# A hybrid decoder step: the state-space convolutions get a buffer of their own, and the norm of the conformer output moves two tiles forward

## The chip, the cores and the metric

One core of a Trainium2 chip. The core has five engines with a queue each: PE (TensorE, matrix products), DVE (VectorE), ACT (ScalarE), POOL (GpSimd) and SP (SyncE, which here only starts transfers). They run side by side and wait for each other through semaphores; each works through its own queue strictly in the order in which the program wrote it. The metric is the device time of one launch in microseconds, lower is better; a kernel's time is the median of its runs.

## What is computed

Two layers (`DEPTH = 2`) of a decoder trunk, over 1024 prompt positions and 8 sequences of 4 sample positions (1056 columns in all). The part around the change:

```python
u = x @ params['w_in'][l]
z, xbc, dt_raw, q, k, v, qi, ki, wi, glu = jnp.split(u, points, axis=-1)
xbc, ssd_conv_new = causal_dwconv(xbc, ssd_conv_prev, ssd_conv_w, ssd_conv_b)   # 4 taps, 768 channels
xbc = jax.nn.silu(xbc)
...
idx, valid = index_select(qi, wi, ki, q_pos, k_top)                             # the best 256 keys of each query
...
gl = glu[..., :CC_WIDTH] * jax.nn.sigmoid(glu[..., CC_WIDTH:])
c, cc_conv_new = causal_dwconv(gl, cc_conv_prev, cc_conv_w, cc_conv_b)          # 31 taps, 256 channels
y_cc = jax.nn.silu(layer_norm(c, cc_ln_g, cc_ln_b))
```

State-space scan, sparse attention, an output projection, two layer norms and a gated feed-forward with a width-3 convolution make up the rest of a layer.

## The kernel before

Activations stay in on-chip memory with channels on the 128 partitions, so a tile is 128 channels by 1056 columns. A layer is a row of stages with a barrier between them (`Stages.end`). The change lies in the third stage, which I call **the projection stage**. In it PE computes 20 tiles of `x @ w_in`, written out as a list of jobs (`IN_ORDER`, `JOBS`, lines 102 to 112):

- two gate and two GLU tiles (gate, GLU, gate, GLU), the input of the conformer convolution;
- XBC0 to XBC5, the input of the state-space ("SSD") convolution;
- Z0 to Z3, the gate of the state-space output;
- K0, K1, Q0, Q1, each followed one tile later by a `rot` job (a product with a rotation matrix, three instructions), which the rotary embedding needs;
- V0 and V1.

Two more jobs belong to the conformer's layer norm: `mean` (a product with a matrix of 1/256) and `var` (the same of the squares). Their places in the list are what lines 105 to 108 decide.

**Two sets of banks.** Job n writes one of two sets of accumulation banks (`n % 2`). PE may start job n only when job n-2 has been read out (`await_freed(pe, n - 2)`). Who reads it out: ACT for XBC, Z, K and Q tiles, DVE for V tiles (two copies) and for `rot` (`rotate`, lines 1678 to 1686: three DVE instructions) and `mean` (`norm_centre`, two subtractions), ACT for `var`.

**What DVE and ACT do beside it.** In the same stage the 256 best keys of each query are found by binary search, 31 bits (`choose`). For each bit DVE finishes the bit before (L1913, L1914), makes the next trial (L1906, L1907), counts two of the sets itself (L1860 to L1910), and ACT counts the other five (L1435). DVE cannot finish a bit before ACT's five counts are done. `BITS_OF_JOB` puts two bits on each tile from the first gate to K0, and one on K1. On ACT the two bits stand behind the tile's read-out.

**Convolutions.** `convolve_by_taps` makes one DVE instruction per tap (L1666 for the first tap, L1668 for the others). The SSD convolution of a tile (4 taps, 1080 columns) is put into `inline` and runs between the tile's two bits. The conformer convolution (`convolve_conformer`, two tiles, 31 taps of 1296 columns) is put into `aside`, a list of work cut into steps. `spend(us, steps)` takes steps from it until their estimated cost (1.35 us a tap, from its width) has used up a budget: 3 after each bit that has no inline work, and at the end of a tile 4 in the XBC and Z tiles. After K1 `aside` holds the rest of the key choice, with 5, 11 and 6 at the end of the later tiles.

**The shared buffer.** The SSD convolutions accumulate in `ACC[1]`, and so does the second conformer tile. Therefore `convolve_conformer` only yields empty steps until Z0 (`ssd_convolved`), and waits for the last SSD `silu`.

On ACT the `mean` job is four activations that add the conformer's bias (L1358, L1359), then two squares (L1274); the `var` job is a square root (L1325), and two activations (L1330) after DVE's reciprocal and scaling (`norm`, L1608, L1612).

Of the kernel before, what the change touches and what calls it, by code (L numbers as in the profile page):

```python
# [24 lines left out]
ACT = mybir.ActivationFunctionType  # L25
AX = mybir.AxisListType

D_MODEL, SEQ, DEPTH, DEC_BATCH, DEC_SEQ, PAST_LEN, PAGE = 1024, 1024, 2, 8, 4, 2048, 128
HEAD, SSD_HEADS, SSD_STATE, SSD_W = 64, 8, 64, 4
# [72 lines left out]
IN_ORDER = [T_GATE, T_GLU, T_GATE + 1, T_GLU + 1] + list(range(T_XBC, T_GATE)) + list(range(T_Z, N_IN))  # L102
for _j in IN_ORDER:

    if _j == T_V:
        JOBS.append(("mean", "cc"))
    if _j == T_V + 1:
        JOBS.append(("var", "cc"))
    JOBS.append(("in", _j))
    if _j - 1 in (T_K, T_K + 1, T_Q, T_Q + 1):  # L110
        JOBS.append(("rot", _j - 1))
# [67 lines left out]
def build(nc, xT, w_in, w_out, w_up, w_down, vec, ln0, const, pages, cache_k, cache_v, cache_kidx,  # L179
          ssm_in, ssd_in, cc_in, ffn_in, yT, kT_out, v_out, ki_out, ssm_p, ssm_s, ssd_out, cc_out, ffn_out):  # L180
    ctx = ExitStack()
    with ctx:
# [33 lines left out]
        def v(col, rows=slice(0, P)):  # L216
            return VEC[rows, col:col + 1]
# [3 lines left out]
        def view(*dims, parts=False):  # L221
            n = int(np.prod(dims))
            a = (WORK_PARTS if parts else WORK)[:, at[0]:at[0] + n]
            at[0] += n
            assert at[0] <= WORK_SIZE, at[0]
            if len(dims) == 2:
                return a.rearrange("p (a b) -> p a b", a=dims[0])
            if len(dims) == 3:
                return a.rearrange("p (a b c) -> p a b c", a=dims[0], b=dims[1])
            return a  # L230
# [38 lines left out]
        at[0] = qi_at  # L269
        ROPE2 = view(TOK)  # L270
        SSDO, CCO = view(6, SSD_H * (1 + DEC_BATCH)), view(2, CC_H * (1 + DEC_BATCH))
        ACC = [MIX[:, 4:6, :].rearrange("p a b -> p (a b)")[:, 0:CC_LEN], view(CC_LEN)]
        assert at[0] <= common

# [222 lines left out]
        def samples(a, seg_len, first, n):  # L497

            return a.rearrange("p (b s) -> p b s", s=seg_len)[:, :, first:first + n]
# [749 lines left out]
        def _(act):  # L1249
# [85 lines left out]
            with act.Fori(0, DEPTH) as layer:  # L1335
# [8 lines left out]
                def silu_xbc(t):  # L1344

                    act.wait_ge(conv_done, t + 1)
                    act.wait_ge(saved, t + 3)
                    act.activation(XBC[:, t, 0:SEQ], ACC[1][:, 0:SEQ], ACT.Silu, bias=v(V_SSDB + t))
                    act.activation(by_sample(XBC[:, t, SEQ:TOK]),
                                   samples(ACC[1][:, SSD_S0:SSD_S0 + DEC_BATCH * SSD_SEG], SSD_SEG, 0, DEC_SEQ),  # L1350
                                   ACT.Silu, bias=v(V_SSDB + t)).then_inc(silu_done, 1)

                def project(n):
# [239 lines left out]
        def _(dve):  # L1593
# [62 lines left out]
            with dve.Fori(0, DEPTH) as layer:  # L1656
# [6 lines left out]
                def convolve_by_taps(acc, src, taps, col, done):  # L1663

                    w = acc.shape[-1]
                    step.then_wait(dve.tensor_scalar(acc, src[:, 0:w], v(col), None, ALU.mult))  # L1666
                    for k in range(1, taps):
                        ins = dve.scalar_tensor_tensor(out=acc, in0=src[:, k:k + w], scalar=v(col + k), in1=acc,  # L1668
                                                       op0=ALU.mult, op1=ALU.add)
                        if k < taps - 1:  # L1670
                            step.then_wait(ins)
                            yield w / 960
                    ins.then_inc(done, 1)
# [11 lines left out]
                                                            op0=ALU.mult, op1=ALU.mult))  # L1685
                    dve.tensor_tensor(raw, raw, ROPE, ALU.add).then_inc(free[n % 2], 1)

                aside, inline, ssd_convolved = [], [], []

                def spend(us, steps):  # L1690

# [6 lines left out]

                def convolve_conformer():
                    for t in range(2):  # L1700
                        while t and not ssd_convolved:
                            yield 1.0
                        if t:
                            dve.wait_ge(silu_done, 6)
                        await_freed(dve, JOB[("in", T_GLU + t)])
                        yield from convolve_by_taps(ACC[t][:, 0:CC_LEN - CC_H], CC[:, t, :], CC_W, V_CCW + t * CC_W,
                                                    cc_convolved)

                def project(n):
# [24 lines left out]
                    elif name[0] == "dup":  # L1734
                        await_full(dve, n)
                        dve.tensor_tensor(KID, job_psum(n), c("cos"), ALU.mult).then_inc(free[n % 2], 1)
                    elif name[0] == "rotdup":
                        await_full(dve, n)
                        dve.tensor_tensor(ROPE1, job_psum(n), c("sin"), ALU.mult).then_inc(free[n % 2], 1)
                        await_freed(dve, n)  # L1740
                        await_freed(dve, n - 1)
                        step.then_wait(dve.tensor_tensor(KID, KID, ROPE1, ALU.add))
                    elif name[0] == "turn":
                        await_full(dve, n)
                        for rows, ch, a, w in ((P, slice(0, NCHUNK), 0, NCHUNK * P),
                                               (NS, slice(NCHUNK, NCHUNK + 1), NCHUNK * P, P)):
                            t = job_psum(n, w, slice(0, rows), first=a).rearrange("p (c m) -> p c m", m=P)
                            dve.tensor_copy(DTT[0:rows, ch, :], t[:, :, DT_ROW:DT_ROW + SSD_HEADS])
                            ins = dve.tensor_scalar(WIT[0:rows, ch, :], t[:, :, WI_ROW:WI_ROW + IDX_HEADS],
                                                    IDX_HEADS ** -0.5, None, ALU.mult)  # L1750
                        ins.then_inc(free[n % 2], 1)
                    elif name[0] == "rot":
                        r = name[1]
                        await_freed(dve, JOB[("in", r)])
                        rotate(QI[:, r - T_QI, :] if r < T_XBC else KTL[:, r - T_K, :] if r < T_Q
                               else QT[:, r - T_Q, :], n, ROPE1 if r < T_XBC else ROPE2,
                               ATT_SCALE if T_Q <= r < T_V else 1.0)
                    elif T_XBC <= name[1] < T_GATE:
                        t = name[1] - T_XBC
                        await_freed(dve, n)  # L1760
                        if t:
                            dve.wait_ge(silu_done, t)
                        inline.append(convolve_by_taps(ACC[1][:, 0:SSD_LEN - SSD_H], XBC[:, t, :], SSD_W,
                                                       V_SSDW + t * SSD_W, conv_done))
                    elif T_GLU <= name[1] < T_Z:
                        t = name[1] - T_GLU
                        await_full(dve, n)
                        if t == 0:
                            dve.wait_ge(hist_set, 1)
                        await_freed(dve, JOB[("in", T_GATE + t)])  # L1770
                        dve.tensor_tensor(CC[:, t, CC_H:CC_S0], job_psum(n, SEQ), MIX[:, 6 + t, 0:SEQ], ALU.mult)
                        dve.tensor_tensor(samples(CC[:, t, CC_S0:], CC_SEG, CC_H, DEC_SEQ),
                                          by_sample(job_psum(n, NS, first=SEQ)), by_sample(MIX[:, 6 + t, SEQ:TOK]),
                                          ALU.mult).then_inc(free[n % 2], 1)
                        if t == 0:
                            aside.append(convolve_conformer())
                    elif name[1] >= T_V:
                        t = name[1] - T_V
                        await_full(dve, n)
                        dve.tensor_copy(VTOK[:, 0:NCHUNK, t * P:(t + 1) * P],  # L1780
                                        job_psum(n, SEQ).rearrange("p (c m) -> p c m", m=P))
                        dve.tensor_copy(VTOK[0:NS, NCHUNK, t * P:(t + 1) * P],
                                        job_psum(n, P, slice(0, NS), first=SEQ)).then_inc(free[n % 2], 1)
# [184 lines left out]
                for n in range(N_IDX, N_A):  # L1968
                    project(n)
                    if JOBS[n][0] == "in":  # L1970
                        j = JOBS[n][1]
                        if j == T_GATE:
                            while next(chosen):
                                pass
                        search(j)
                        if j == T_Z:
                            ssd_convolved.append(True)
                        if j == LAST_BITS:
                            aside.append(chosen)
                        spend(4 if j < T_K else 0 if j == T_K else 5 if j < T_Q else 11 if j < T_V else 6, aside)  # L1980
                stage.end()


# [456 lines left out]
```

## Time and profile before

| | before |
|---|---|
| median of three runs | 3820.9 us (3813.37, 3820.9, 3825.1) |
| the profiled execution | 3816.51 us, its span 3814.7 us |
| PE busy | 3304.1 us, 87% of the span |
| DVE busy | 1909.9 us, 50% |
| ACT busy | 1236.7 us, 32% |
| mean granted clock of PE | 0.919 of full speed |

Busy time is an average over stages with different limits. PE at 87% says that most of the launch is bound by products; the projection stage, about 370 us in each of the two layers, is one in which PE, DVE and ACT take turns in waiting. The profiled execution lies 4.4 us below the median of the runs. In the rows below, a timeline row has start, duration, engine, line, operation, result and inputs, shape and count; the bracket is the idle time of the engine ahead of it and who ended it.

### The profile page before, as it was taken

To read this page: it belongs to the slowest core of one execution; us is meant where nothing else is said; L and a number is where in the kernel's file an instruction comes from. 1 tells how busy PE (TensorE), PEld (TensorE's weight loads), DVE (VectorE), ACT (ScalarE), POOL (GpSimd) and SP (SyncE) were. 2 spreads that over 40 slices of the span, in tenths; PEclk is the share of its full clock that TensorE was granted. 3 is DMA by queue.
4 is the path that set the end of the run, shared out by engine and by line. 5 is a ranking of instruction groups with operands and counts; after the bars stand their busy time and mean duration, and the time that the engine had idled before them with its cause. 6 is when DMAs were issued, how large, how long until landed. Compare 5 with 4: busy or idle time off the path is not lost.

```text
span 3814.7 us, 51646 instructions
## 1 busy us (share of the span) xinstructions
PE 3304.1 (87%) x19286; PEld 2652.2 (70%) x19286; DVE 1909.9 (50%) x2976; ACT 1236.7 (32%) x2251; POOL 638.6 (17%) x651
## 2 busy tenths in 40 slices
PE   4899887857889999999868998786669999999995
PEld 2454455624789999999834453564349899999994
DVE  4467864332475434334435868633226645335335
ACT  3246623333252112212223574243333412112213
POOL 0000000001013333333100000000110333334331
PEclk8999998857999999999989998897589999999998
DMA  3111104304301111111021110142151111111111
GB/s 100 49 36 29 32 17 124 94 17 123 102 17 35 52 48 37 53 50 34 27 81 48 34 34 23 62 117 63 35 155 40 34 45 36 54 45 37 55 34 58
DMA packets 169894, 206.59 MB, mean 54 GB/s; under 512 B 61025, under 2 KB 138146, under 8 KB 168738
## 3 DMA queue, kind: packets, MB, share of 16 engines
q1 hardware_dynamic: 143138, 185.36, 16.4%
q10 hardware_dynamic: 26496, 17.84, 1.6%
q8 instruction: 154, 2.52, 0.3%
q14 instruction: 106, 0.87, 0.1%
HBM read 187.17 MB, written 15.96 MB: 53 GB/s over the span
## 4 chain that ended last, share of the span: by engine, by line
PE 64%; DVE 16%; ACT 9%; SPq 5%; issue 3%; DMA 2%; POOL 0%; ACTq 0%; DVEq 0%; POOLq 0%
PE PS L742 41%; PE PS L723 7%; DVE WORK L1668 4%; DVE MIX L1668 2%; ACT WORK L1435 2%; PE PS L755 2%; PE PS L827 2%; ACT X L1306 2%; SPq L424 2%; SPq L425 2%; DVE WORK L1860 1%; PE PS L935 1%; DMA RING<-cache_k 1%; PE PS L781 1%; DVE WORK L1632 1%
## 5 line engine op out<-in xcount | busy, mean ns | idle before, releaser
L742 PE MATMUL PS<-WORK_parts,WHIGH_parts 128*128 128x352 f32 x4224 | 869.5, 328 | 35.2 <-POOL WORK_parts L709 17.7
L723 PE MATMUL PS<-X,RING 128*128 128x512 f32 (+1 forms) x2016 | 671.8, 496 | 109.3 <-DMA RING<-w_in 65.4
L742 PEld LDWEIGHTS PS<-WORK_parts,WHIGH_parts 128*128 128x128 f32 x4224 | 724.2, 191 | 38.9 <-issue 20.6
L742 PE MATMUL PS<-WORK_parts,RING_parts 128*128 128x352 f32 x3168 | 691.3, 327 | 0.0
L723 PEld LDWEIGHTS PS<-X,RING 128*128 128x128 f32 x2016 | 338.4, 194 | 443.8 <-issue 375.2
L742 PEld LDWEIGHTS PS<-WORK_parts,RING_parts 128*128 128x128 f32 x3168 | 545.4, 190 | 0.0
L1668 DVE SCALAR_TENSOR_TENSOR WORK<-WORK,VEC 128x1072 f32<-128x1072 f32 (+2 forms) x272 | 525.6, 1932 | 9.7
L1252 ACT ACTIVATE WORK<-PS 128x32 f32<-128x32 f32 (+11 forms) x412 | 190.8, 514 | 842.1 <-PE PS L742 579.7
L489 POOL TENSOR_TENSOR RING_parts<-RING,WHIGH_parts 128x1024 fp32r<-128x1024 f32 (+2 forms) x184 | 372.0, 2022 | 467.2 <-ACT WHIGH_parts L1252 466.9
L742 PE MATMUL PS<-X_parts,WHIGH_parts 128*128 128x352 f32 x2016 | 434.4, 323 | 0.0
L1435 ACT ACTIVATE WORK<-WORK 128x512 bf16<-128x512 f32 x310 | 285.7, 922 | 198.5 <-DVE WORK L1907 198.4
L1666 DVE TENSOR_SCALAR WORK<-WORK,VEC 128x1072 f32<-128x1072 f32 (+2 forms) x102 | 80.0, 784 | 529.8 <-ACT WORK L1252 529.4
L742 PEld LDWEIGHTS PS<-X_parts,WHIGH_parts 128*128 128x128 f32 x2016 | 344.4, 188 | 0.0
L1252 ACT ACTIVATE WHIGH_parts<-RING 128x1024 fp32r<-128x1024 f32 (+2 forms) x188 | 155.5, 827 | 442.6 <-PE PS L742 420.0
L2264 DVE TENSOR_TENSOR MIX<-MIX,PS 128x1056 f32<-128x1056 f32 x80 | 100.3, 1253 | 286.9 <-PE PS L742 286.9
L755 PE MATMUL PS<-WORK_parts 128*128 128x352 f32 x576 | 144.2, 330 | 0.0
L2077 DVE CUSTOM_DVE_ANT_0 WORK<-PS,WORK 128x384 f32<-128x384 f32 (+5 forms) x48 | 42.4, 883 | 201.8 <-PE PS L1084 201.8
L709 POOL TENSOR_TENSOR WORK_parts<-WORK,WORK_parts 128x1056 fp32r<-128x1056 f32 x44 | 108.3, 2462 | 167.6 <-ACT WORK_parts L1252 167.6
L1252 ACT ACTIVATE WORK_parts<-WORK 128x1056 fp32r<-128x1056 f32 (+1 forms) x56 | 59.4, 1078 | 217.9 <-DVE WORK L2252 217.9
L935 PE MATMUL PS<-CONST,RING 128*128 128x128 f32 x512 | 83.0, 305 | 49.5 <-DMA RING<-cache_k 30.7
L1860 DVE TENSOR_SCALAR_CACHE_REDUCE WORK<-WORK 128x544 bf16<-128x544 f32 (+6 forms) x164 | 115.9, 742 | 0.3
L935 PEld LDWEIGHTS PS<-CONST,RING 128*128 128x128 f32 x512 | 62.3, 155 | 67.9 <-DMA RING<-cache_k 37.0
(318 smaller groups left out, 3722.2 us busy)
## 6 DMA issues: line engine op xcount, KB each, us to landing
RING<-w_up SPq DMA_DIRECT2D x88, 512.0 KB, 3.6
RING<-cache_k SPq DMA_DIRECT2D x200, 128.0 KB, 2.2
RING<-cache_v SPq DMA_DIRECT2D x192, 128.0 KB, 2.1
RING<-w_in SPq DMA_DIRECT2D x46, 512.0 KB, 3.6
RING<-w_down SPq DMA_DIRECT2D x80, 256.0 KB, 2.7
RING<-cache_v ACTq DMA_DIRECT2D x64, 128.0 KB, 2.5
RING<-cache_k ACTq DMA_DIRECT2D x56, 128.0 KB, 2.6
yT<-X SPq DMA_DIRECT2D x5, 1408.0 KB, 5.5
```

What stands on the lines that cost most here:

```text
L489: eng.tensor_tensor(low, raw, WHIGH[:, m % 2, 0:w].bitcast(F32), ALU.subtract).then_inc(done, 1)
L709: pool.tensor_tensor(HIDL[:, b, :], HID[:, b, :], HIDH[:, b, :].bitcast(F32), ALU.subtract).then_inc(hid_low, 1)
L723: mm = pe.matmul(job_psum(n, w, first=first), stationary(k), moving(k)[:, first:first + w], start=k == 0, stop=k == k_tiles - 1)
L742: mm = pe.matmul(thirds(n)[:, third, :], a, x[:, third * THIRD:(third + 1) * THIRD], start=k == 0 and part == 0, stop=k == tiles - 1 and p ...
L755: mm = pe.matmul(dst, a[:, w], third_of(x, t), start=k == 0 and part == 0, stop=k == KT - 1 and part == 2)
L935: mm = pe.transpose(key_bank(k)[:, (j % 2 * 2 + t) * P:(j % 2 * 2 + t + 1) * P], cache_page(name)[:, j, t * P:(t + 1) * P], c("ident"))
L1252: return act.activation(dst, src, ACT.Copy)
L1435: ins = act.activation(SCAN_ASIDE[s][:, 0:w], SEL[:, SEL_AT[i]:SEL_AT[i] + w], ACT.Sign, bias=SCAN_TRIED[:, s:s + 1], scale=SCAN_SCALE, ac ...
L1666: step.then_wait(dve.tensor_scalar(acc, src[:, 0:w], v(col), None, ALU.mult))
L1668: ins = dve.scalar_tensor_tensor(out=acc, in0=src[:, k:k + w], scalar=v(col + k), in1=acc, op0=ALU.mult, op1=ALU.add)
L1860: marks.append(step.mark(dve.tensor_scalar(ASIDE[len(marks) % 2][:, 0:x.shape[-1]], x, limit, None, op, ALU.add, accum_out=to)))
L2264: dve.tensor_tensor(y, y, thirds(n), ALU.add).then_inc(free[n % 2], 1)
```

## The change

The SSD convolutions accumulate in `SSD_ACC`, a part of `MIX` that is unused until Z2 is read out. The second conformer tile no longer waits: `ssd_convolved` and the wait for `silu_done` are gone. The budget at the end of an XBC tile is 7 instead of 4 (six conformer taps instead of three). `mean` stands ahead of Q0 instead of V0, `var` ahead of Q1 instead of V1. Nothing else changes, but since `n % 2` counts jobs, the moves also change which job's banks a later job waits for.

```diff
--- before.py
+++ after.py
@@ -102,9 +102,9 @@
 IN_ORDER = [T_GATE, T_GLU, T_GATE + 1, T_GLU + 1] + list(range(T_XBC, T_GATE)) + list(range(T_Z, N_IN))
 for _j in IN_ORDER:
-    if _j == T_V:
+    if _j == T_Q:
         JOBS.append(("mean", "cc"))
-    if _j == T_V + 1:
+    if _j == T_Q + 1:
         JOBS.append(("var", "cc"))
     JOBS.append(("in", _j))
     if _j - 1 in (T_K, T_K + 1, T_Q, T_Q + 1):
@@ -269,6 +269,7 @@
         at[0] = qi_at
         ROPE2 = view(TOK)
         SSDO, CCO = view(6, SSD_H * (1 + DEC_BATCH)), view(2, CC_H * (1 + DEC_BATCH))
+        SSD_ACC = MIX[:, 2:4, :].rearrange("p a b -> p (a b)")[:, 0:SSD_LEN]
         ACC = [MIX[:, 4:6, :].rearrange("p a b -> p (a b)")[:, 0:CC_LEN], view(CC_LEN)]
         assert at[0] <= common
@@ -1345,9 +1346,9 @@
                     act.wait_ge(conv_done, t + 1)
                     act.wait_ge(saved, t + 3)
-                    act.activation(XBC[:, t, 0:SEQ], ACC[1][:, 0:SEQ], ACT.Silu, bias=v(V_SSDB + t))
+                    act.activation(XBC[:, t, 0:SEQ], SSD_ACC[:, 0:SEQ], ACT.Silu, bias=v(V_SSDB + t))
                     act.activation(by_sample(XBC[:, t, SEQ:TOK]),
-                                   samples(ACC[1][:, SSD_S0:SSD_S0 + DEC_BATCH * SSD_SEG], SSD_SEG, 0, DEC_SEQ),
+                                   samples(SSD_ACC[:, SSD_S0:SSD_S0 + DEC_BATCH * SSD_SEG], SSD_SEG, 0, DEC_SEQ),
                                    ACT.Silu, bias=v(V_SSDB + t)).then_inc(silu_done, 1)
                 def project(n):
@@ -1685,7 +1686,7 @@
                                                             op0=ALU.mult, op1=ALU.mult))
                     dve.tensor_tensor(raw, raw, ROPE, ALU.add).then_inc(free[n % 2], 1)
-                aside, inline, ssd_convolved = [], [], []
+                aside, inline = [], []
                 def spend(us, steps):
@@ -1698,10 +1699,6 @@
                 def convolve_conformer():
                     for t in range(2):
-                        while t and not ssd_convolved:
-                            yield 1.0
-                        if t:
-                            dve.wait_ge(silu_done, 6)
                         await_freed(dve, JOB[("in", T_GLU + t)])
                         yield from convolve_by_taps(ACC[t][:, 0:CC_LEN - CC_H], CC[:, t, :], CC_W, V_CCW + t * CC_W,
                                                     cc_convolved)
@@ -1760,7 +1757,7 @@
                         await_freed(dve, n)
                         if t:
                             dve.wait_ge(silu_done, t)
-                        inline.append(convolve_by_taps(ACC[1][:, 0:SSD_LEN - SSD_H], XBC[:, t, :], SSD_W,
+                        inline.append(convolve_by_taps(SSD_ACC[:, 0:SSD_LEN - SSD_H], XBC[:, t, :], SSD_W,
                                                        V_SSDW + t * SSD_W, conv_done))
                     elif T_GLU <= name[1] < T_Z:
                         t = name[1] - T_GLU
@@ -1973,11 +1970,9 @@
                             while next(chosen):
                                 pass
                         search(j)
-                        if j == T_Z:
-                            ssd_convolved.append(True)
                         if j == LAST_BITS:
                             aside.append(chosen)
-                        spend(4 if j < T_K else 0 if j == T_K else 5 if j < T_Q else 11 if j < T_V else 6, aside)
+                        spend(7 if T_XBC <= j < T_GATE else 4 if j < T_K else 0 if j == T_K else 5 if j < T_Q else 11 if j < T_V else 6, aside)
                 stage.end()
```

How the order moves on the engines (line numbers of the changed kernel are one higher up to line 1690, three lower behind 1780):

DVE, the end of tile XBC1: behind the second bit's own counts (L1860 to L1910) and ahead of the next tile's first bit (L1913). Before:

```order
L1860 TENSOR_SCALAR WORK<-WORK 128x544 [waits vector_step]
L1860 TENSOR_SCALAR WORK<-WORK 128x384 [waits vector_step]
L1873 STREAM_TRANSPOSE WORK<-WORK 128x32 [waits vector_step]
L1874 TENSOR_REDUCE WORK<-WORK 128x8 [waits vector_step]
L1875 COPY WORK<-WORK 128x32 [waits vector_step]
L1877 STREAM_TRANSPOSE WORK<-WORK 128x32 [waits vector_step]
L1910 TENSOR_TENSOR WORK<-WORK 128x7 [waits vector_step]
L1913 TENSOR_TENSOR WORK<-WORK 128x5 [waits silu_done,scan_counted,bank_set_free0,vector_step]
L1914 COPY_PREDICATED WORK<-WORK 128x7 [waits vector_step]
```

With the change (L1669 is the conformer tap, the others as above):

```order
L1857 TENSOR_SCALAR WORK<-WORK 128x544 [waits vector_step]
L1857 TENSOR_SCALAR WORK<-WORK 128x384 [waits vector_step]
L1870 STREAM_TRANSPOSE WORK<-WORK 128x32 [waits vector_step]
L1871 TENSOR_REDUCE WORK<-WORK 128x8 [waits vector_step]
L1872 COPY WORK<-WORK 128x32 [waits vector_step]
L1874 STREAM_TRANSPOSE WORK<-WORK 128x32 [waits vector_step]
L1907 TENSOR_TENSOR WORK<-WORK 128x7 [waits vector_step]
L1669 SCALAR_TENSOR_TENSOR WORK<-WORK,VEC 128x1296 [waits vector_step] x9
L1910 TENSOR_TENSOR WORK<-WORK 128x5 [waits silu_done,scan_counted,bank_set_free0,vector_step]
L1911 COPY_PREDICATED WORK<-WORK 128x7 [waits vector_step]
```

Nine conformer taps now stand in the queue ahead of XBC2's first bit, where there were none. The same nine stand at the end of XBC2, five at the end of XBC3, and at the end of XBC0 eleven (a first tap, L1667, among them) in place of three; the tiles Z0 to Z3 have none left.

PE, behind the K1 tile. `WORK,CONST` is a `rot` job (the first three rows: that of K0), `X,RING` a projection tile (here Q0), `MIX,MEAN` the job `mean`. Before:

```order
L723 MATMUL PS<-WORK,CONST 128x512 [waits bank_set_free0]
L723 MATMUL PS<-WORK,CONST 128x512
L723 MATMUL PS<-WORK,CONST 128x32
L723 MATMUL PS<-X,RING 128x512 [waits bank_set_free1,slot_loaded1]
L723 MATMUL PS<-X,RING 128x512 x15
L723 MATMUL PS<-X,RING 128x32 x8
L723 MATMUL PS<-WORK,CONST 128x512 [waits bank_set_free0,bank_set_free1]
```

With the change:

```order
L724 MATMUL PS<-WORK,CONST 128x512 [waits bank_set_free0]
L724 MATMUL PS<-WORK,CONST 128x512
L724 MATMUL PS<-WORK,CONST 128x32
L724 MATMUL PS<-MIX,MEAN 128x512 [waits bank_set_free1,cc_ready]
L724 MATMUL PS<-MIX,MEAN 128x512 x3
L724 MATMUL PS<-MIX,MEAN 128x32 x2
L724 MATMUL PS<-X,RING 128x512 [waits bank_set_free0,slot_loaded1]
```

`mean`, which waits for ACT's bias activations (`cc_ready`), now stands ahead of Q0. Q0's banks are those of K0's `rot` (`bank_set_free0`), which DVE frees by rotating; they were those of K1 (`bank_set_free1`), which ACT frees by a copy.

PE, the end of the stage. `RING,X` is a V tile, `L801` the job `var`, the `WORK,CONST` rows are the `rot` job of Q1. Before:

```order
L723 MATMUL PS<-WORK,CONST 128x512 [waits bank_set_free1]
L723 MATMUL PS<-WORK,CONST 128x512
L723 MATMUL PS<-WORK,CONST 128x32
L801 MATMUL PS<-MIX,MEAN 128x512 [waits norm_squared,bank_set_free0]
L801 MATMUL PS<-MIX,MEAN 128x512
L801 MATMUL PS<-MIX,MEAN 128x32
L801 MATMUL PS<-MIX,MEAN 128x512 [waits norm_squared]
L801 MATMUL PS<-MIX,MEAN 128x512
L801 MATMUL PS<-MIX,MEAN 128x32
L827 MATMUL PS<-RING,X 128x128 [waits bank_set_free1,slot_loaded0]
```

With the change:

```order
L828 MATMUL PS<-RING,X 128x128 [waits bank_set_free1,slot_loaded3]
L828 MATMUL PS<-RING,X 128x128 x63
L828 MATMUL PS<-RING,X 32x128 x8
L724 MATMUL PS<-WORK,CONST 128x512 [waits bank_set_free0,bank_set_free1]
L724 MATMUL PS<-WORK,CONST 128x512
L724 MATMUL PS<-WORK,CONST 128x32
L828 MATMUL PS<-RING,X 128x128 [waits bank_set_free1,slot_loaded0]
```

V1 (last row of before, last row with the change) took the banks of Q1's `rot` job, which DVE frees; it now takes those of V0.

## Rows read from the trace of the kernel before

**Rows 1.** Timeline of PE, first layer's projection stage.

```profile
315.02 15.68 PE L723 MATMUL PS<-X,RING 128*128 128x512 f32 x48 [2.29 <-ACT WORK L1252]
...
379.68 62.49 PE L723 MATMUL PS<-X,RING 128*128 128x512 f32 x192 [0.15 <-ACT WORK L1252]
...
445.05 18.05 PE L723 MATMUL PS<-X,RING 128*128 128x512 f32 x48 [2.88 <-ACT MIX L1378]
...
483.75 17.48 PE L723 MATMUL PS<-X,RING 128*128 128x512 f32 x48 [15.44 <-ACT WORK L1252]
...
501.06 2.10 PE L723 MATMUL PS<-WORK,CONST 128*128 128x512 f32 x6
...
522.33 4.07 PE L723 MATMUL PS<-MIX,MEAN 128*128 128x512 f32 x12 [1.70 <-ACT MIX L1359]
...
526.23 16.40 PE L827 MATMUL PS<-RING,X 128*128 128x128 f32 x144
...
556.27 17.73 PE L827 MATMUL PS<-RING,X 128*128 128x128 f32 x144 [7.71 <-DVE WORK L1686]
```

**Rows 2.** Timeline of PE, second layer: Q0 and V1.

```profile
2356.75 17.94 PE L723 MATMUL PS<-X,RING 128*128 128x512 f32 x48 [14.14 <-ACT WORK L1252]
...
2429.73 17.95 PE L827 MATMUL PS<-RING,X 128*128 128x128 f32 x144 [7.71 <-DVE WORK L1686]
```

**Rows 3.** Timeline of DVE in tiles XBC0 to XBC4.

```profile
311.42 4.78 DVE L1668 SCALAR_TENSOR_TENSOR MIX<-WORK,VEC,MIX 128x1296 f32<-128x1296 f32 x3
...
317.64 0.17 DVE L1913 TENSOR_TENSOR WORK<-WORK 128x5 int32<-128x5 f32 x1 [1.45 <-ACT WORK L1349]
...
320.69 0.78 DVE L1666 TENSOR_SCALAR WORK<-WORK,VEC 128x1080 f32<-128x1080 f32 x1
...
325.53 0.15 DVE L1913 TENSOR_TENSOR WORK<-WORK 128x5 int32<-128x5 f32 x1
...
333.48 0.16 DVE L1913 TENSOR_TENSOR WORK<-WORK 128x5 int32<-128x5 f32 x1 [4.94 <-ACT WORK L1349]
...
365.14 0.17 DVE L1913 TENSOR_TENSOR WORK<-WORK 128x5 int32<-128x5 f32 x1 [4.94 <-ACT WORK L1349]
```

**Rows 4.** Timeline of DVE, first bits of tiles Z2 and Z3.

```profile
430.59 0.16 DVE L1913 TENSOR_TENSOR WORK<-WORK 128x5 int32<-128x5 f32 x1
...
451.13 0.17 DVE L1913 TENSOR_TENSOR WORK<-WORK 128x5 int32<-128x5 f32 x1
```

**Rows 5.** Timeline of DVE, from the 31st bit to the stage's end.

```profile
488.39 0.17 DVE L1913 TENSOR_TENSOR WORK<-WORK 128x5 int32<-128x5 f32 x1 [2.60 <-ACT WORK L1435]
...
494.71 1.26 DVE L1682 SCALAR_TENSOR_TENSOR WORK<-WORK,CONST 128x1056 f32<-128x1056 f32 x1
...
556.26 6.75 DVE L1608 RECIPROCAL WORK<-WORK 128x1056 f32<-128x1056 f32 x1
...
574.03 1.22 DVE L1780 COPY WORK<-PS 128x1024 f32<-128x1024 f32 x1 [8.56 <-PE PS L827]
...
585.65 0.63 DVE L1956 TENSOR_SCALAR WORK<-WORK 128x896 f32<-128x896 f32 x1
```

**Rows 6.** Groups by shape: conformer taps of both tiles; busy us, mean ns.

```profile
L1668 DVE SCALAR_TENSOR_TENSOR WORK<-WORK,VEC 128x1296 f32<-128x1296 f32 x60 | 94.2, 1569 | 2.1
...
L1668 DVE SCALAR_TENSOR_TENSOR MIX<-WORK,VEC,MIX 128x1296 f32<-128x1296 f32 x60 | 94.1, 1569 | 2.1
```

**Rows 7.** Timeline of ACT in the same stage.

```profile
378.45 1.08 ACT L1252 ACTIVATE WORK<-PS 128x1024 f32<-128x1024 f32 x2
...
477.97 0.72 ACT L1435 ACTIVATE WORK<-WORK 128x512 bf16<-128x512 f32 x1 [0.92 <-DVE WORK L1907]
...
482.58 1.02 ACT L1252 ACTIVATE WORK<-PS 128x1056 f32<-128x1056 f32 x1
...
519.67 1.14 ACT L1358 ACTIVATE MIX<-MIX,VEC 128x1024 f32<-128x1024 f32 x1
```

**Rows 8.** Windows: from:to, length, busy of PE, PEld, DVE, ACT, POOL, granted clock, DMA.

```profile
445.00:463.00 18.00, 17.95 (x48) 8.86 (x48) 17.20 (x34) 7.89 (x17) 0.00 (x0) 0.87 0.02 7
```

## The prediction

> **What bounds the kernel now.** I read the timeline of PE through the projection stage first, since PE is 87% busy: there only its idle times can be won. Its waits name who held it, and for each of them I went to that engine's timeline.
>
> PE [rows 1]: a projection tile takes 62.49/4 = 15.6 us, a V tile 16.3, a `rot` job 2.0, `mean` and `var` 4.1 each. The first eight tiles run nearly closed up. Then PE waits 2.88 us ahead of K1, 15.44 ahead of Q0 (ended by ACT, which had to finish bits before it could copy K1), 1.70 ahead of `mean` and 7.71 ahead of V1 (DVE had to rotate Q1 first). The second layer has 14.14 and 7.71 at the same places [rows 2].
>
> DVE shows where that comes from. In the XBC tiles it runs 317.64 to 333.48, 15.84 us a tile, and sits idle 4.94 us of it, waiting for ACT [rows 3]; PE, at 15.6, is just behind. In the Z tiles, where the second conformer tile now runs, a tile takes 451.13 - 430.59 = 20.5 us [rows 4], 5 more than PE's; the lateness gathered there is the 15.44 us ahead of Q0. So the limit changes hands: a DVE-ACT loop in the XBC tiles that is as fast as PE, DVE in the Z tiles.
>
> The end of the stage: after V1's product DVE works from 574.03 to 585.65 + 0.63 = 586.28 [rows 5], 12.3 us, and the next stage starts on that. So the stage's length follows V1's end on PE one for one.
>
> **The change, step by step** (first layer, times on the clock of the trace of before).
>
> *The buffer itself.* Taps cost 1569 ns into either memory, so the move of the SSD sums costs nothing [rows 6]; with its gap a tap takes 1.60, a first tap 0.93 (estimated from 0.78 for 1080 columns [rows 3] as 0.78 x 1296/1080).
>
> *The taps pulled into the XBC tiles.* XBC0: DVE had three taps from 311.42 to 316.2, then waited until 317.64. Now a first tap and seven others follow: 316.2 + 0.93 + 7 x 1.60 = 328.3, a lag of 10.7 against before. XBC1 and XBC2: from the first bit to the second 325.53 - 317.64 = 7.89; the second bit 320.69 - 317.64 = 3.05; nine taps 14.4; together 25.3 in place of 15.84, a lag of 9.5 each, because only three of nine taps fit into the 4.94 us of idle time. XBC3 with five taps: 7.89 + 3.05 + 8.0 = 18.9, 3.1 more. The sum is 10.7 + 9.5 + 9.5 + 3.1 = 32.8: XBC4, whose first bit was at 365.14 [rows 3], starts at 397.9. From there on nothing is aside, and the loop is that of before, 32.8 late.
>
> ACT's read-out of XBC5, at 378.45 [rows 7], is what lets Z1 start on PE at 379.68 [rows 1]. ACT's read-outs stand behind the bits in its queue, and the bits wait for DVE's trial. So Z1 starts at 379.68 + 32.8 = 412.5. The PE idle time of this stretch is new: about 12, 8 to 10 and 8 to 10 us ahead of XBC4, XBC5 and Z0 (lags of 10.7, 20.2 and 29.7 at their read-outs), 1 ahead of Z1.
>
> *What the Z tiles give back.* DVE now has only bits there. ACT's counts take 482.58 - 477.97 = 4.61 and wait 0.92 for the next trial [rows 7]: about 5.6 a bit, and 2 x 5.6 + 1.0 for the read-out = 12.3 us, under PE's 15.6. So PE runs Z1, Z2, Z3, K0, K1 closed up: 412.5 + 5 x 15.6 = 490.5 (before: 445.05 + 18.05 = 463.1), K0's `rot` to 492.5.
>
> *The norm two tiles sooner.* ACT reads K1 (1.0), counts the 31st bit (4.6) and adds the bias (519.67 to 522.33, 2.7 [rows 1, 7]): 490.6 + 8.3 = 498.9. `mean` starts there, PE having waited 6.5, and ends at 503.1. On DVE the key choice's step behind the 31st bit stands ahead of K0's rotation: 488.39 to 494.71, 6.3 [rows 5]; then three instructions of 1.26, 3.8 in all. From the end of the 31st count at 496.3 this gives 496.4 + 6.3 + 3.8 = 506.5, and Q0 now needs those banks: it starts at 506.6, PE having waited another 3.5. Before it started at 483.75, so the lag is 22.9: 10 of the 32.8 are back.
>
> *From Q0 to the end.* A wait costs clock. After 2.29 us of idle XBC3 still took 15.68; after 2.88 K1 took 18.05, with a granted clock of 0.87 over 445 to 463 [rows 1, 8]: part of it at the lower level of 1.2 GHz. Q0's 3.5 us is nearest to the second, so I charge 2.2 of the possible 0 to 2.4. Then 506.6 + 17.8 = 524.4; K1's `rot` 526.4; `var` 530.5 (its squares were done by 512); Q1 needs K1's rotation, 526.5 + 3.8 = 530.3, just in time, to 546.1; Q0's `rot` 548.1; V0 564.4; Q1's `rot` 566.4; V1, which needs only V0's copies (1.5 us) and no rotation, 566.4 + 16.3 = 582.7. V0 needs Q1 read out, and ACT is by then in the norm: 530.6 + 1.1 + DVE's reciprocal 6.75 [rows 5] + two scalings 2.5 + two activations 2.4 = 543.4, 2.7 us to spare. In before V1 ended at 556.27 + 17.73 = 574.0. The stage ends 8.7 us later. What is saved here is the 7.71 and 1.70 of waits, and `mean` (4.1), which moved ahead of Q0.
>
> The tail of 12.3 us is unchanged: the budgets behind K1 and the steps they take are the same. POOL's and SP's queues hold the same instructions in the same order.
>
> **The sum.** 8.7 us a layer, twice: +17.4 us on the profiled 3816.5 is 3833.9. That execution lies 4.4 below the median; the four times known average 3819.0, and 3819.0 + 17.4 gives **3836 us**.
>
> The Trainium skill, "TensorE: Matmul & The Clock Gate", section "Part 1: The HAM clock gate (the "warmup" mystery)", says that the array's clock is halved unless recent activity has released it. The loss behind K1's wait agrees [rows 1, 8]; by it the same loss would stand behind every long new wait. That is rival C; where such a start is covered, the sum does not change.
>
> **The rivals.**
>
> *A, faster.* The taps hide in the XBC tiles and the late Z tiles are simply gone. Each us of lag at XBC4 is one us at V1, so break-even is a lag of 32.8 - 8.7 = 24.1, and with no lag the time is 3819 + 2 x (8.7 - 32.8) = 3771. For it: PE's four named waits are 27.7 us a layer. Against it: the idle time in an XBC tile is 4.94 us and the new taps are 14.4; a lag of 24 would need taps of 1.3 us. Chance 0.05.
>
> *B, no difference to speak of.* The waits around `mean` come out shorter: the 6.5 and 3.5 stand in a row on three engines (ACT's count and bias, DVE's step and rotation), and without the 2.2 of clock and some 2 us of these it is +4.5 a layer, 3828. A full loss of these two waits and of the clock, 12.2, would give 3819 - 7 = 3812, still within 0.3%. For it: the 3.5 is a difference of long sums. Against it: each of the orders is fixed by a queue. Chance 0.20.
>
> *C, slower than I say.* The clock is lost at more places: each slow start costs up to 2.4 [rows 1]. In the XBC tiles this is covered, since XBC4 (342.7 + 18.0) ends long before XBC5 may start, and Z0 (393.5 + 18.0 = 411.5) 1 us before Z1; ahead of `mean` it is covered by DVE's rotation, which ends 3.4 us later. If Z0 or V1 fall behind too, it is 2.4 to 4.8 a layer: 3841 to 3846. Chance 0.12.
>
> *D, the norm holds V0.* If DVE reached the reciprocal over 2.7 us late, V0 would slip. Its queue holds only K1's rotation there. It would add what exceeds 2.7; I count it into C.
>
> **Chances and range.** The forecast as worked out, +13 to +20: 0.63. A 0.05, B 0.20, C and D 0.12. What a measurement of this kernel can tell from no change is about 0.3%, 11.5 us. Faster by more than that: A, 0.05. Slower: the forecast, C and D, 0.75, less 0.01 for its edge; within 0.3%: B, and that edge, 0.21. The range leaves out A, the lower half of B and the top of C: 3823 to 3847. Its low end is +4 (the clock unpaid, and B's cut in the waits), its high end C's.
>
> **What would show it.** In the profile of the changed kernel: tiles XBC1 and XBC2 last 25 us on DVE between first bits, with nine taps each; PE waits about 12, 9, 9 us ahead of XBC4, XBC5 and Z0, ended by ACT; the Z tiles run closed up at 15.6; two waits of about 6.5 and 3.5 stand around `mean`; none ahead of V1; V1 ends near 583 and the stage near 595. Wrong would be: XBC tiles of 16 to 18 us, Q0 starting before 500, or a stage that ends before 586. A fault of size would sit first in the 3.5 ahead of Q0 and in the clock behind it.

## The result and the profile after

The changed kernel takes 3833.8 us, the median of 20 runs, against 3818.0 for the kernel before on the same chips: a ratio of 1.0037, 95% interval 1.0027 to 1.0046. It is slower by 10 to 18 us, on the side and at about the size that was forecast (+17.4 us, 3836). The profiled execution took 3835.1 us, its span 3833.3.

PE's timeline in the projection stage, first layer, then second. This execution reaches the stage 1.96 us sooner than that of before (201.94 against 203.90); "aligned" below means that 1.96 is added.

```profile
201.94 108.83 PE L724 MATMUL PS<-X,RING 128*128 128x512 f32 x336 [0.91 <-DVEq L454]
...
340.80 18.05 PE L724 MATMUL PS<-X,RING 128*128 128x512 f32 x48 [12.09 <-ACT WORK L1253]
366.17 17.31 PE L724 MATMUL PS<-X,RING 128*128 128x512 f32 x48 [7.32 <-ACT WORK L1253]
391.53 18.28 PE L724 MATMUL PS<-X,RING 128*128 128x512 f32 x48 [8.05 <-ACT WORK L1253]
410.35 78.00 PE L724 MATMUL PS<-X,RING 128*128 128x512 f32 x240 [0.54 <-ACT WORK L1253]
...
496.57 7.04 PE L724 MATMUL PS<-MIX,MEAN 128*128 128x512 f32 x12 [6.28 <-ACT MIX L1360]
504.43 15.68 PE L724 MATMUL PS<-X,RING 128*128 128x512 f32 x48 [0.82 <-DVE WORK L1687]
...
526.15 15.68 PE L724 MATMUL PS<-X,RING 128*128 128x512 f32 x48 [0.22 <-DVE WORK L1687]
...
561.89 16.40 PE L828 MATMUL PS<-RING,X 128*128 128x128 f32 x144
592.45 0.66 PE L978 MATMUL PS<-WORK,CONST 128*128 128x64 f32 x2 [14.16 <-DVE WORK L1988]
```

```profile
2085.07 108.83 PE L724 MATMUL PS<-X,RING 128*128 128x512 f32 x336 [0.91 <-DVEq L454]
...
2223.94 18.55 PE L724 MATMUL PS<-X,RING 128*128 128x512 f32 x48 [10.69 <-ACT WORK L1253]
...
2293.48 79.45 PE L724 MATMUL PS<-X,RING 128*128 128x512 f32 x240 [1.72 <-ACT WORK L1253]
...
2381.16 6.82 PE L724 MATMUL PS<-MIX,MEAN 128*128 128x512 f32 x12 [6.28 <-ACT MIX L1360]
2389.02 15.68 PE L724 MATMUL PS<-X,RING 128*128 128x512 f32 x48 [1.03 <-DVE WORK L1687]
...
2477.03 0.66 PE L978 MATMUL PS<-WORK,CONST 128*128 128x64 f32 x2 [14.16 <-DVE WORK L1988]
```

The first row of the stage and the first of the next one, in both layers of the kernel before:

```profile
203.90 108.83 PE L723 MATMUL PS<-X,RING 128*128 128x512 f32 x336 [0.91 <-DVEq L453]
...
588.16 0.66 PE L977 MATMUL PS<-WORK,CONST 128*128 128x64 f32 x2 [14.17 <-DVE WORK L1993]
...
2076.92 108.83 PE L723 MATMUL PS<-X,RING 128*128 128x512 f32 x336 [0.92 <-DVEq L453]
...
2461.84 0.66 PE L977 MATMUL PS<-WORK,CONST 128*128 128x64 f32 x2 [14.17 <-DVE WORK L1993]
```

Against [rows 1, 2]: the waits of 15.44 ahead of Q0 and 7.71 ahead of V1 are gone, the tiles Z1 to K1 run closed up, that is without waits (78.00/5 = 15.6), and in place of those waits stand 12.09, 7.32 and 8.05 us ahead of XBC4, XBC5 and Z0 and 6.28 ahead of `mean`. The last row of each layer is the first product of the next stage. From the first gate tile to it, the stage is 592.45 - 201.94 = 390.5 us long, before 588.16 - 203.90 = 384.3; in the second layer 392.0 against 384.9. That is 13.3 us for both layers.

DVE's timeline of the same stretch: first bits of the XBC tiles, with the conformer taps ahead of them.

```profile
326.28 0.16 DVE L1910 TENSOR_TENSOR WORK<-WORK 128x5 int32<-128x5 f32 x1
...
337.20 14.41 DVE L1669 SCALAR_TENSOR_TENSOR WORK<-WORK,VEC 128x1296 f32<-128x1296 f32 x9
351.65 0.17 DVE L1910 TENSOR_TENSOR WORK<-WORK 128x5 int32<-128x5 f32 x1
...
362.57 14.40 DVE L1669 SCALAR_TENSOR_TENSOR WORK<-WORK,VEC 128x1296 f32<-128x1296 f32 x9
377.00 0.16 DVE L1910 TENSOR_TENSOR WORK<-WORK 128x5 int32<-128x5 f32 x1
...
395.83 0.15 DVE L1910 TENSOR_TENSOR WORK<-WORK 128x5 int32<-128x5 f32 x1
...
411.65 0.16 DVE L1910 TENSOR_TENSOR WORK<-WORK 128x5 int32<-128x5 f32 x1 [4.94 <-ACT WORK L1350]
```

XBC1 and XBC2 last 25.4 us each (15.84 in [rows 3]), with nine taps and no idle time left. XBC4, a tile without taps, has its 4.94 back (last row).

Two windows, `mean` and Q0 (length, busy time of PE, PEld, DVE, ACT, POOL, then the granted clock):

```profile
496.50:503.60 7.10, 7.03 (x12) 3.13 (x12) 6.89 (x14) 0.02 (x1) 0.00 (x0) 0.57 0.00 0
504.40:520.00 15.60, 15.57 (x49) 7.95 (x49) 12.12 (x28) 2.17 (x2) 0.00 (x0) 1.00 0.01 1
```

The clock was lost in `mean`, granted 0.57 and so mostly at the lower level of 1.2 GHz; Q0 behind it ran at full speed. The Trainium skill, "TensorE: Matmul & The Clock Gate", section "Part 1: The HAM clock gate (the "warmup" mystery)", says that a clock lowered by idle time is released again by activity; the two windows agree.

### The profile page after: what moved, and what is told of

It is laid out like the page before. It is cut to its first block, busy times and chain, and to the rows that moved or that the text cites. A ratio compares the mean times of both kernels' runs of the same rounds, so it can differ in the third digit from the quotient of the medians.

```text
span 3833.3 us, 51646 instructions
## 1 busy us (share of the span) xinstructions
PE 3320.1 (87%) x19286; PEld 2660.3 (69%) x19286; DVE 1909.4 (50%) x2976; ACT 1237.1 (32%) x2251; POOL 646.7 (17%) x651
## 4 chain that ended last, share of the span: by engine, by line
PE 68%; DVE 15%; ACT 6%; SPq 4%; issue 3%; DMA 3%; POOL 0%; ACTq 0%; DVEq 0%; POOLq 0%
PE PS L743 41%; PE PS L724 11%; DVE MIX L1669 4%; DVE WORK L1669 3%; PE PS L756 2%; PE PS L828 2%; ACT X L1307 2%; SPq L425 1%; SPq L426 1%; PE PS L936 1%; DVE WORK L1857 1%; DMA RING<-cache_k 1%; PE PS L782 1%; DVE WORK L1633 1%; ACT WORK L1475 1%
## 5 line engine op out<-in xcount | busy, mean ns | idle before, releaser
L1669 DVE SCALAR_TENSOR_TENSOR WORK<-WORK,VEC 128x1072 f32<-128x1072 f32 (+1 forms) x236 | 477.3, 2022 | 8.4
L1667 DVE TENSOR_SCALAR WORK<-WORK,VEC 128x1072 f32<-128x1072 f32 (+1 forms) x90 | 70.6, 784 | 530.9 <-ACT WORK L1253 530.9
L1669 DVE SCALAR_TENSOR_TENSOR MIX<-WORK,VEC,MIX 128x1296 f32<-128x1296 f32 (+1 forms) x96 | 142.5, 1484 | 3.4
```

## The experiments

Nine kernels, in three groups; the kernels of a group and the kernel before shared a chip. Its median there was 3821.7 us in the first group, 3828.7 in the second and 3820.9 in the third, so ratios are compared across groups. The stage lengths are read from one profile each, as above.

| kernel | ratio to before, 95% | stage, layer 1 / 2, us |
|---|---|---|
| before | 1 | 384.3 / 384.9 |
| the change | 1.0037 (1.0027 to 1.0046) | 390.5 / 392.0 |
| 6 taps in an XBC tile | 0.9996 (0.9985 to 1.0008) | 385.6 / 384.3 |
| 3 taps in an XBC tile | 0.9899 (0.9886 to 0.9912) | 366.1 / 366.5 |
| 9 taps, norm late | 1.0032 (1.0018 to 1.0046) | 394.3 / 392.0 |
| norm early, nothing else | 0.9988 (0.9976 to 0.9999) | 382.9 / 382.9 |
| buffer alone | 1.0001 (0.9989 to 1.0013) | 385.1 / 385.1 |
| 3 taps, norm late | 0.9895 (0.9878 to 0.9911) | 367.2 / 367.1 |
| 3 taps, none behind Z tiles | 0.9875 (0.9859 to 0.9890) | 363.5 / 363.5 |
| the same, norm one tile sooner than before, key choice pulled forward | 0.9829 (0.9814 to 0.9844) | 354.2 / 355.5 |
| the same, 2 taps a bit in Z tiles | 0.9808 (0.9794 to 0.9821) | 348.6 / 348.6 |

### The budget in the XBC tiles: 6 taps, and 3

```diff
-spend(7 if T_XBC <= j < T_GATE else 4 if j < T_K ...
+spend(4 if T_XBC <= j < T_GATE else 4 if j < T_K ...     # first kernel
+spend(0 if T_XBC <= j < T_GATE else 4 if j < T_K ...     # second kernel
```

> The changed kernel with one number undone: the budget behind a tile XBC is 4 again in place of 7, so 6 conformer taps and not 9 fall into each XBC tile. Theory (taps beyond DVE's 4.94 us of idle time in an XBC tile are the loss): each tile runs over by 6 x 1.60 - 4.94 = 4.7 us in place of 9.5; all six together leave Z0 some 26 us late in place of 33, so 6 to 7 us a layer of the 6.3 and 7.0 lost come back: 3816 to 3823 us where the kernel before has 3818. XBC1 to XBC4 last 20.5 us each on DVE between first bits. Rival N (the loss is the norm ahead of Q0, with its waits of 6.28 and 0.82 and a mean of 7.04 us): nothing changes there, 3830 to 3837.

> The changed kernel with the budget behind a tile XBC set to 0: only the 3 taps of the second bit stay in each XBC tile, 4.8 us against 4.94 of idle time. Theory: XBC tiles last 15.8 to 16.2 us as in the kernel before, some 15 taps are done there for nothing and 15 are left for Z0 and Z1; K1 ends near where it did before (463), mean waits 6 and takes 7, Q0 starts near 480, and from there 73.9 us to V1's end as in the changed kernel: 554 in place of 574, 18 to 20 us a layer, 3778 to 3784 us, faster than both. Rival N (the norm ahead of Q0 is the loss): at most what e1 gives back, 3816 or more. A second rival (the buffer of its own costs by itself, whatever the number of taps): 3830 or more.

Measured: 3818.5 and 3783.4 us. DVE in one XBC tile, with 6 taps:

```profile
344.02 0.16 DVE L1910 TENSOR_TENSOR WORK<-WORK 128x5 int32<-128x5 f32 x1
...
354.95 9.60 DVE L1669 SCALAR_TENSOR_TENSOR WORK<-WORK,VEC 128x1296 f32<-128x1296 f32 x6
364.58 0.17 DVE L1910 TENSOR_TENSOR WORK<-WORK 128x5 int32<-128x5 f32 x1
```

and with 3:

```profile
332.30 0.16 DVE L1910 TENSOR_TENSOR WORK<-WORK 128x5 int32<-128x5 f32 x1
...
343.23 4.78 DVE L1669 SCALAR_TENSOR_TENSOR WORK<-WORK,VEC 128x1296 f32<-128x1296 f32 x3
348.14 0.17 DVE L1910 TENSOR_TENSOR WORK<-WORK 128x5 int32<-128x5 f32 x1
```

The tile lasts 15.84 us with 3 taps, 20.56 with 6 and 25.36 with 9. The first three are free; the next three cost 1.57 us each, (20.56 - 15.84)/3, and the last three their whole 1.60, (25.36 - 20.56)/3. Both rivals fall: the same early norm and the same buffer stand in a kernel 1% faster than before. PE in the kernel with 3 taps:

```profile
430.56 32.99 PE L724 MATMUL PS<-X,RING 128*128 128x512 f32 x96 [4.87 <-ACT MIX L1379]
...
471.88 5.67 PE L724 MATMUL PS<-MIX,MEAN 128*128 128x512 f32 x12 [6.39 <-ACT MIX L1360]
479.75 15.68 PE L724 MATMUL PS<-X,RING 128*128 128x512 f32 x48 [2.19 <-DVE WORK L1687]
```

The waits around `mean` stand there as in the changed kernel; only the lag ahead of them is gone.

### The norm: left late, and moved alone

```diff
-    if _j == T_Q:           # the changed kernel, norm back
+    if _j == T_V:
         JOBS.append(("mean", "cc"))
```

The other kernel has the reverse edit in the kernel before; `var` moves with `mean` in both.

> The changed kernel with mean and var moved back ahead of V0 and V1; buffer and budget 7 stay. Theory: the lag of 32.8 us in the XBC tiles stays, the two waits around mean go and the waits of 1.70 ahead of mean and 7.71 ahead of V1 come back: Q0 starts at 490 and V1 ends 88.4 to 90.3 us behind it as in the kernel before, 578.6 to 580.6, against 578.3 in the changed kernel: 0 to 2.3 us a layer, 3834 to 3839 us. Rival N: the loss goes, 3817 to 3821 us.

> The kernel before with mean and var moved ahead of Q0 and Q1 as in the change, and nothing else. Theory: the waits of 15.4 ahead of Q0 and of 7.7 ahead of V1 become waits around mean: mean starts near 491, Q0 near 498.5 behind DVE's rotation of K0, and V1 ends 73.9 us later, 572.4 against 574.0: 0 to 2 us a layer less, 3813 to 3819 us. Rival N: 6 to 7 us a layer more, 3830 to 3833 us.

Measured: 3834.0 and 3816.1 us. Left late, PE's timeline shows the old waits behind the lag:

```profile
493.62 15.68 PE L724 MATMUL PS<-X,RING 128*128 128x512 f32 x48
...
530.40 4.07 PE L724 MATMUL PS<-MIX,MEAN 128*128 128x512 f32 x12 [1.69 <-ACT MIX L1360]
...
564.96 19.08 PE L828 MATMUL PS<-RING,X 128*128 128x128 f32 x144 [7.71 <-DVE WORK L1687]
```

Moved alone, the wait of 15.44 us becomes one of 22.52:

```profile
490.85 5.72 PE L723 MATMUL PS<-MIX,MEAN 128*128 128x512 f32 x12 [22.52 <-ACT MIX L1359]
498.71 15.68 PE L723 MATMUL PS<-X,RING 128*128 128x512 f32 x48 [2.15 <-DVE WORK L1686]
```

So the norm's place is worth 0 to 2 us a layer, a little to the good by itself. The rival that it is the loss falls twice. The first layer of the kernel with the norm late is 3.8 us longer than that of the change, where 0 to 2.3 were expected; the second layers are equal. In the first, Z1 to K1 took 79.45 us for 78.00, and V1 took 19.08 behind its wait for 17.73 in the kernel before.

### The buffer alone

```diff
                     for t in range(2):
+                        while t and not ssd_convolved:
+                            yield 1.0
```

The norm is late here too. The lines that end the empty steps behind Z0 are put back as well; the budget of 7 stays, but finds only empty steps in XBC1 to XBC5.

> The buffer alone: the SSD sums stand in MIX and the wait on ACT's sixth silu is gone, but the conformer's second tile still starts behind Z0, and mean and var stand ahead of V0 and V1 as before. Theory (taps cost the same into either memory, 1.58 us and 1.35 us; nothing else hangs on the buffer): no change, ratio to the kernel before 0.999 to 1.001, waits of 15.4 ahead of Q0 and 7.7 ahead of V1 as before. Rival (the buffer's place itself costs, as DVE, ACT and PE share it with the reads of MIX): the XBC tiles last over 16.2 us on DVE, and the ratio is 1.002 or more.

Measured: 3821.2 us beside 3820.9. PE waits 14.14 and 14.15 us ahead of Q0 in the two layers and 7.71 ahead of V1. For Q0 15.4 were expected in the first layer; Q0 starts 279.84 us into the stage there and 279.85 in the kernel before, and the wait is shorter because K0's `rot` ahead of it took 4.02 us in place of 2.72. The XBC tiles last 15.84 us on DVE, as before. The buffer is free, and by itself it brings nothing.

### Norm late with 3 taps

> The kernel with budget 0 in the XBC tiles (3783 us), and mean and var moved back ahead of V0 and V1. Theory (the norm's place is worth next to nothing, also where the taps are hidden): Q0 then starts right behind K0's rot at 465.5 in place of 479.8, but V1 ends 88.4 to 90.4 us behind Q0's start in place of 73.9, so 553.9 to 555.9 in place of 553.6: 0 to 2.3 us a layer more, 3783 to 3788 us. Rival (with the taps hidden the early norm is what makes the gain): some of the 7 to 20 us a layer come back, 3800 us or more.

Measured: 3787.1 us, a ratio of 0.9895 against 0.9899. The stages are 1.1 and 0.5 us longer with the norm late. Also where the taps are hidden, the norm's place is worth next to nothing.

### No budget behind the Z tiles

```diff
-spend(0 if T_XBC <= j < T_GATE else 4 if j < T_K else 0 if j == T_K ...
+spend(4 if j < T_XBC or T_GATE <= j < T_Z else 0 if j < T_Q - 1 ...
```

> The kernel with budget 0 in the XBC tiles, and the budget 0 in the Z tiles and K0 too: only the taps behind the bits are left, 6 in a Z tile. Theory (per tile, what exceeds PE's 15.6 us is lost, what stays under is free): Z0 and Z1 then take about 2 x (2.84 + 4.8) = 15.3 us on DVE in place of 20.1, the wait of 4.87 us ahead of K0 goes, and 3 to 5 us a layer with it: 3773 to 3778 us. Rival (only the sum of the work of DVE up to K1 counts, and the wait comes back at mean): 3782 to 3785 us.

Measured: 3780.2 us, a ratio of 0.9875 against 0.9899; the two intervals overlap, so the times alone leave open how much of it is the change. The profiles say more: the stage is 2.5 us shorter in the first layer and 3.0 in the second, between the rival and the low end of the theory. PE now runs closed up from XBC4 to K1, and the wait that stood ahead of K0 comes back in large part ahead of `mean`: K1 ends 6.5 us sooner in the stage, and `mean` waits 10.38 in place of 6.39.

```profile
334.86 126.01 PE L724 MATMUL PS<-X,RING 128*128 128x512 f32 x384 [2.48 <-ACT WORK L1253]
...
473.20 6.87 PE L724 MATMUL PS<-MIX,MEAN 128*128 128x512 f32 x12 [10.38 <-ACT MIX L1360]
```

A second chain runs beside PE's: the bits on DVE and ACT, at whose end ACT is free for the norm's bias. DVE's first row of each bit in the Z tiles, at first with three taps behind a bit, further on with none:

```profile
407.31 0.17 DVE L1910 TENSOR_TENSOR WORK<-WORK 128x5 int32<-128x5 f32 x1
410.36 4.78 DVE L1669 SCALAR_TENSOR_TENSOR WORK<-WORK,VEC 128x1296 f32<-128x1296 f32 x3
415.17 0.16 DVE L1910 TENSOR_TENSOR WORK<-WORK 128x5 int32<-128x5 f32 x1
...
437.04 0.16 DVE L1910 TENSOR_TENSOR WORK<-WORK 128x5 int32<-128x5 f32 x1
442.65 0.17 DVE L1910 TENSOR_TENSOR WORK<-WORK 128x5 int32<-128x5 f32 x1 [2.60 <-ACT WORK L1436]
```

A bit takes 7.86 us with three taps and 5.61 with none, of which DVE waits 2.60 for ACT's counts. In the Z tiles, too, a tap is free only inside that.

### A version that beats both, and two taps a bit

The norm's `mean` stands ahead of Q1 and `var` ahead of V0, and the steps of the key choice are pulled forward:

```diff
-else 5 if j < T_Q else 11 if j < T_V else 6, aside)
+else 14 if j < T_V else 10 if j == T_V else 6, aside)    # K1: 0
```

> A version to beat both: buffer of its own, budgets 0 in XBC, Z and K tiles, mean ahead of Q1 and var ahead of V0 (one tile sooner than before), and the key choice's steps pulled forward with budgets of 14, 14 and 10 behind Q0, Q1 and V0, so that little of the 12.3 us of DVE work behind V1 is left. Theory: 3 to 5 us a layer as in the run with budget 0 in the Z tiles, 2 to 4 from the norm's waits, and 6 to 9 of the tail: 11 to 18 a layer under 3783, 3747 to 3761 us. Rival (the steps pulled forward stand ahead of a rotation that PE waits for): no more than the first of these, 3773 us or above.

Measured: 3764.1 us beside 3828.7, above the 3747 to 3761 expected; but the kernel before was 7 us slower here than on the chip of the 3783. In ratios it is 0.9829 against 0.9899 with budget 0 in the XBC tiles: 0.7% or 27 us less, 13 a layer, in the range of the theory. The sum came out, its terms did not. In the first layer, against that kernel, K1 ends 6.6 us sooner in the stage (3 to 5 were expected from the Z tiles), from there to V1's end it is 3.0 us less (2 to 4 expected of the norm's waits), and the tail gave 2.3 in place of 6 to 9: PE's wait at the stage's end fell only from 14.16 to 11.91 us, since the largest of the key choice's sets (1024 columns), which had run after the stage, now came into it. So the stages of this kernel, and of the one with two taps a bit, hold work that the others do later. The norm's place and the key choice's steps change together here, and no run parts them. What was left was a wait ahead of Q0, from the chain of bits:

```profile
465.81 17.37 PE L724 MATMUL PS<-X,RING 128*128 128x512 f32 x48 [3.34 <-ACT WORK L1253]
```

```diff
-                        spend(3, inline or aside)
+                        spend(3 if inline or j < T_Z else 2, inline or aside)
```

> The best version so far with one number changed: in the Z tiles 2 conformer taps behind a bit in place of 3. Theory, as mended by the run with budget 0 in the Z tiles (the chain of bits, 5.62 us each with no tap and 7.86 with three, sets when K1 can be read and when the norm's bias is free; a tap is free only inside the 2.6 us for which DVE waits for ACT in each bit): 14 taps then cost 7 x 0.43 = 3.0 us in place of about 10, the 31st bit is 6 to 7 us sooner, the wait of 3.34 us ahead of Q0 goes, and the 1.7 to 2.9 us that Q0 loses behind it: 4 to 6 us a layer, 8 to 12 us, ratio to the kernel before 0.980 to 0.981 against 0.983. Rival (only the number of taps counts, 14 in both): ratio 0.983.

Measured: 3747.1 us, 0.9808, as the mended theory expected. Q0 follows K0's `rot` without a wait, and takes 15.68:

```profile
461.05 2.10 PE L724 MATMUL PS<-WORK,CONST 128*128 128x512 f32 x6
462.99 15.68 PE L724 MATMUL PS<-X,RING 128*128 128x512 f32 x48
```

DVE, one bit with two taps:

```profile
406.51 0.17 DVE L1910 TENSOR_TENSOR WORK<-WORK 128x5 int32<-128x5 f32 x1
409.56 3.17 DVE L1669 SCALAR_TENSOR_TENSOR WORK<-WORK,VEC 128x1296 f32<-128x1296 f32 x2
412.77 0.16 DVE L1910 TENSOR_TENSOR WORK<-WORK 128x5 int32<-128x5 f32 x1
```

That bit lasts 6.26 us, 0.65 more than one without taps, where 0.43 were expected; so the 31st bit comes 5.2 us sooner in the stage and not 6 to 7. The same 14 taps, spread thinner, take 0.21% off, 8 us. The two intervals overlap a little (one begins at 0.9814, the other ends at 0.9821), but the profiles agree: the stages are 5.6 and 6.9 us shorter. This is 1.9% under the kernel before.

## Why the prediction was right, step by step

- **The buffer costs nothing.** Right, and shown by itself (1.0001). A tap takes 1569 to 1570 ns into either buffer in the changed kernel too.
- **The lag of 32.8 us.** Right. XBC1 and XBC2 lag by 9.5 each (25.36 - 15.84). XBC4's first bit is at 395.83, aligned 397.8; forecast 397.9. The runs with 3, 6 and 9 taps show that the lag is the loss, and that it begins where the taps use up the idle 4.94 us; the runs with the norm late and the buffer alone leave no other. The waits ahead of XBC5 and Z0, 7.32 and 8.05 us, are under the 8 to 10 forecast, since the tile ahead of each ran 1.6 to 2.4 us longer than 15.68: the sum of the two is what the lag sets.
- **What the Z tiles give back.** Right. K1 ends at 488.35, aligned 490.3; forecast 490.5.
- **The waits around `mean`.** The first is right (6.28 against 6.5). The second was given as 3.5 and is 0.82, because `mean` took 7.04 us and not 4.1. The two together, with `mean` between, are 14.14 us against 14.1, so Q0 starts at aligned 506.4; forecast 506.6.
- **The 2.2 us of clock at Q0: the step that was mis-sized.** It was charged to Q0, by likeness to K1's start. It fell on `mean`, which stood behind the longer wait and was covered by DVE's rotation of K0. Q0 took 15.68, at a granted clock of 1.00. From Q0's end on all is some 2.3 us sooner than forecast: V1 ends at aligned 580.3 for 582.7, and the stage is 6.3 us longer for 8.7; 7.0 in the second layer.
- **The norm's price.** That V0 would not be held is right: there is no wait ahead of it. Ahead of V1 there is none either.
- **The sum.** 13.3 us in the two stages for 17.4. The two profiled spans differ by 18.6; the other 5.3 lie in stretches in which the two kernels are the same, and one profile of each does not tell their cause. The medians of 20 runs differ by 15.8. That this comes within 2 us of 17.4 is in part luck: the stages give 4 less than forecast, and something outside them, which the prediction does not have, makes up for part of it.

Of the rivals, A (the taps hide) is refuted at nine taps and true at three; its break-even was put at a lag of 24.1 us, and with six taps Z0's first bit on DVE is 25.3 us late (419.74 for 394.48 in the kernel before) and the time even. B's smaller losses account for what the forecast had too much: the clock went unpaid at Q0. D did not happen. A small piece of C happened, at another tile than C names: in the second layer Z1, behind a wait of 1.72 us, started at a granted clock of 0.90 (2293.4 to 2310.0), Z1 to K1 took 79.45 us for 78.00, and the second stage is longer than the first by just these 1.45 (391.96 for 390.51). In the first layer the slow starts of XBC4, XBC5 and Z0 (18.05, 17.31, 18.28 us) were covered by the waits for DVE and ACT, as argued.

## What to carry to other kernels

When side work is moved into another tile, compare it with the idle time of the engine in that one tile and not with the sum: here 4.8 us of taps a tile cost nothing, and every tap beyond cost its full 1.6 us. The buffer alone was worth nothing and the norm's place about 0 to 2 us a layer; what the buffer makes possible, the second tile's taps in pieces of the size of the idle time, was worth 17 to 18 us a layer with 3 taps in an XBC tile. Pieces that nearly fit (two taps, 3.2 us, where DVE waited 2.6 a bit) in place of three gave another 6 to 7 in the stage. A wait that goes at one place can come back at the next end of a chain if the chain itself is not made shorter: ahead of `mean` it was 22.52 us with the norm moved alone, and 10.38 where the wait ahead of K0 had been taken away.

## What the runs showed of the hardware

In these profiles the clock lost to a wait was paid by what PE ran first behind it. In five of them `mean` stood there and took 5.7 to 7.0 us in place of 4.1, and Q0, right behind it, took 15.68 each time. Where Q0 itself stood behind the wait, it took 17.37 (a wait of 3.34 us, the version with the key choice pulled forward) and 17.48 (15.44 us, the kernel before). The price did not follow the wait's length: in the first layer of the changed kernel behind 12.09, 7.32 and 8.05 us the tiles took 18.05, 17.31 and 18.28.

The kernel's budgets count a tap at 1.35 us, its columns over 960 per us; it takes 1.57. Between 1080 and 1296 columns a tap grows by 1569 - 1344 = 225 ns, 1.04 ns a column, so some 0.22 us of it is fixed, if the columns count alike (an estimate from two shapes). The same operation in the key choice (L1948, 16-bit data, same kernel and stage) takes 618 ns for 384 columns and 1151 for 896, which gives the same two numbers. Its groups by shape in the changed kernel's first projection stage (busy us, mean ns):

```profile
L1669 DVE SCALAR_TENSOR_TENSOR WORK<-WORK,VEC 128x1296 f32<-128x1296 f32 x30 | 47.1, 1570 | 1.1
L1669 DVE SCALAR_TENSOR_TENSOR MIX<-WORK,VEC,MIX 128x1296 f32<-128x1296 f32 x30 | 47.1, 1569 | 1.1
...
L1669 DVE SCALAR_TENSOR_TENSOR MIX<-WORK,VEC,MIX 128x1080 f32<-128x1080 f32 x18 | 24.2, 1344 | 0.6
```

The Trainium skill, "VectorE: DVE Perf Modes", section "The TRN2 errata — SBUF-src ops pay a fixed extra latency per instruction", says that VectorE instructions with on-chip sources pay a fixed cost each; these rows agree with one of 0.22 us.
